# A two-layer decoder trunk on one core: the modulation product goes from VectorE to TensorE in four column groups

## The reference

```python
c_act = jax.nn.silu(c)
for l in range(DEPTH):
    mod = (c_act @ ada_w[l] + ada_b[l])[:, None, :]
    sh1, sc1, gt1, sh2, sc2, gt2 = jnp.split(mod, N_MOD, axis=-1)
    h = rms_norm(x, norm1_g[l]) * (1.0 + sc1) + sh1
    x = x + gt1 * token_mixer(h, ...)      # latent attention, differential attention, convolution, gates, w_o
    h = rms_norm(x, norm2_g[l]) * (1.0 + sc2) + sh2
    x = x + gt2 * conv_gated_mlp(h, ...)   # w_up, 3-tap convolution, silu gate, w_down
return rms_norm(x, final_g)
```

## Time and profile before

| | |
|---|---|
| median of 3 runs | 1114.99 us (1114.21 to 1120.05) |
| profiled execution | 1116.03 us, span in the trace 1114.2 us |
| TensorE busy | 1006.3 us, 90% of the span |
| VectorE busy | 869.1 us, 78% |
| ScalarE busy | 515.3 us, 46% |
| mean granted TensorE clock | 0.956 of full speed |
| DMA | 201.07 MB, 180 GB/s on average |

### The profile page before, as it was taken

One profiled execution on the slowest core, in us unless ns is written; L12 is line 12 of the kernel. 1 busy time (PEld: TensorE's weight loads), 2 busy tenths in 40 slices (PEclk: granted clock), 3 DMA queues, 4 the chain that ended last, 5 costly groups with the idle time before them and its releaser, 6 DMA issues.

```text
span 1114.2 us, 20254 instructions
## 1 busy us (share of the span) xinstructions
PE 1006.3 (90%) x7601; PEld 961.3 (86%) x7601; DVE 869.1 (78%) x1235; ACT 515.3 (46%) x715; POOL 17.3 (2%) x18
## 2 busy tenths in 40 slices
PE   2599999989888999999969999998997989999997
PEld 1598888989888999999969888898997989999996
DVE  5848989988696788898655898998869578888643
ACT  1644355437433554553345435543734355545432
POOL 6000000000000000000000000000000000000000
PEclk9898999889999899999989999987999989999998
DMA  9664443437656366657755444343666545564540
GB/s 318 239 189 152 124 131 100 153 104 249 241 195 222 115 207 221 218 188 299 265 178 187 155 124 126 105 148 109 229 232 220 185 145 199 196 218 155 187 152 38
DMA packets 138942, 201.07 MB, mean 180 GB/s; under 512 B 3416, under 2 KB 114148, under 8 KB 138852
## 3 DMA queue, kind: packets, MB, share of 16 engines
q1 hardware_dynamic: 138501, 199.63, 53.3%
q10 hardware_dynamic: 351, 0.26, 0.1%
HBM read 198.83 MB, written 1.05 MB: 179 GB/s over the span
## 4 chain that ended last, share of the span: by engine, by line
PE 62%; DVE 18%; issue 13%; ACT 2%; DMA 2%; SPq 1%; DVEq 1%; ACTq 0%
PE PB L1236 13%; PE PB L1237 12%; PE PB L1238 12%; DVE wL L838 4%; PE MI L1198 2%; PE SC L1236 2%; PE SC L1237 2%; PE SC L1238 2%; DVE buf L922 2%; DVE acc L793 2%; PE ST L1205 1%; DMA raw<-in_w_in 1%; DVE rdev L979 1%; PE SC L1337 1%; DVE xn L1025 1%
## 5 line engine op out<-in xcount | busy, mean ns | idle before, releaser
L1236 PE MATMUL PB<-hH,wH 128*128 128x256 f32 (+1 forms) x1568 | 467.8, 298 | 43.3 <-DVE hL L855 24.4
L1237 PE MATMUL PB<-hL,wH 128*128 128x256 f32 (+1 forms) x1568 | 451.8, 288 | 0.0
L1238 PE MATMUL PB<-hH,wL 128*128 128x256 f32 (+1 forms) x1568 | 451.5, 288 | 0.0
L838 DVE TENSOR_TENSOR wL<-raw,wH 128x2048 fp32r<-128x2048 f32 (+3 forms) x152 | 320.5, 2111 | 83.4 <-ACT wH L564 80.8
L1236 PEld LDWEIGHTS PB<-hH,wH 128*128 128x128 f32 (+1 forms) x1568 | 308.1, 197 | 57.2 <-issue 17.3
L564 ACT ACTIVATE wH<-raw 128x2048 fp32r<-128x2048 f32 (+3 forms) x152 | 266.4, 1769 | 132.1 <-DMA raw<-in_w_down 55.4
L1237 PEld LDWEIGHTS PB<-hL,wH 128*128 128x128 f32 (+1 forms) x1568 | 309.0, 197 | 3.3 <-issue 2.9
L1238 PEld LDWEIGHTS PB<-hH,wL 128*128 128x128 f32 (+1 forms) x1568 | 308.3, 197 | 0.0
L922 DVE SCALAR_TENSOR_TENSOR buf<-G,vec,buf 128x256 f32<-128x256 f32 x240 | 98.0, 477 | 0.3
L1075 DVE SCALAR_TENSOR_TENSOR cb<-PB,vec,cb 128x255 f32<-128x255 f32 (+1 forms) x88 | 36.3, 475 | 23.9 <-ACT cb L711 21.2
L796 DVE SCALAR_TENSOR_TENSOR acc<-ada,c_act,acc 128x1024 f32<-128x1024 f32 x40 | 51.4, 1284 | 2.3 <-DVE acc L793 1.2
(11 more groups left out here) (251 smaller groups left out, 1675.1 us busy)
## 6 DMA issues: line engine op xcount, KB each, us to landing
raw<-in_w_in SPq DMA_DIRECT2D x48, 1024.0 KB, 5.6
raw<-in_w_up SPq DMA_DIRECT2D x44, 1024.0 KB, 5.0
ada<-in_ada_w SPq DMA_DIRECT2D x40, 1024.0 KB, 5.7
raw<-in_w_down SPq DMA_DIRECT2D x22, 1024.0 KB, 5.0
ada_pre<-in_ada_w SPq DMA_DIRECT2D x8, 1024.0 KB, 11.6
raw<-in_w_o SPq DMA_DIRECT2D x8, 1024.0 KB, 6.2
raw<-in_w_out_diff SPq DMA_DIRECT2D x4, 1024.0 KB, 5.4
raw<-in_w_out_conv SPq DMA_DIRECT2D x4, 1024.0 KB, 6.0
```

Source lines behind the costliest of these rows:

```text
L838: dve.tensor_tensor(wL[s][:, 0:size], raw[s][:, 0:size], wH[s][:, 0:size].bitcast(F32), ALU.subtract).then_inc(w_lo[s], 1)
L1236: pe.matmul(out, a, xh(k), start=first and k == 0, stop=False, skip_group_check=True)
L1237: pe.matmul(out, a, xl(k), start=False, stop=False, skip_group_check=True)
L1238: ins = pe.matmul(out, b, xh(k), start=False, stop=last and k == kt - 1, skip_group_check=True)
```

## The change

The product moves to TensorE. Its weights are `c_col`, a 128x32 tile per block of rows whose column 0 holds the factors and whose other 31 columns are zero; the moving operand is the loaded block in halves of 512 columns. One load gives four matmuls, each in its own group of 32 columns of the array (`tile_position`), so each writes its own 32 partitions of `MI`; four loads accumulate there. ScalarE then copies `MI` (128x512) to `ada_rows`, and TensorE turns and adds the rows with four matmuls (`ada_rows` as weights, two columns of zeros and ones). VectorE's products, `acc` and its clearing go. VectorE still adds the bias, now near the front of a step rather than at its end. Four entries of the table move by one step, so that a part starts after the bias of the last is added. TensorE's loop over the four rounds of `w_up` is written out.

```diff
-ADA_STEPS = [1, 4, 7, 24, 26, 28, 30, 32, 34, 36, 38, 40] + [None] * 4 + [60, 62, 64, 66, 68, 70, 72, 74]
+ADA_STEPS = [1, 4, 7, 24, 27, 28, 30, 32, 35, 36, 38, 40] + [None] * 4 + [61, 62, 64, 66, 69, 70, 72, 74]
...
         @block.scalar
+            def ada_evict(count):
+                act.wait_ge(ada_used, count)
+                act.activation(ada_rows[:, :], MI[:, :], ACT.Copy).then_inc(ada_out, 1)
...
+            ada_evict(ADA_PART)
             root(0, 0)
+            ada_evict(2 * ADA_PART)
             high(0, 0)
...
             def mixer_step(l, n):
+                ada_evict_at(l, n)
                 high(l, n + 2)
...
         @block.vector
-                if first:
-                    ins = dve.tensor_scalar(acc[:, :], src[:, 0, :], factor[:, 0:1], None, ALU.mult)
-                else:
-                    ins = dve.scalar_tensor_tensor(acc[:, :], src[:, 0, :], factor[:, 0:1], acc[:, :], ALU.mult, ALU.add)
-                ins.then_inc(ada_half, 1)
-                dve.wait_ge(ada_half, halves)
-                dve.scalar_tensor_tensor(acc[:, :], src[:, 1, :], factor[:, 1:2], acc[:, :], ALU.mult,
-                                         ALU.add).then_inc(ada_used, 1)
...
                 if n < OUTS:
                     low(l, n + 2)
+                ada_work(l, n)
...
-                dve.memset(acc[:, :], 0.0).then_inc(acc_clear, 1)
...
         @block.tensor
-                for m in range(DT):
-                    ins = pe.matmul(MI[:, m:m + 1], acc[:, m * P:(m + 1) * P], ones[:, 0:1], start=True, stop=True)
+            def ada_products(src, i):
+                for k in range(2):
+                    for half in range(2):
+                        q = 2 * k + half
+                        ins = pe.matmul(MI[32 * q:32 * q + 32, :], c_col[:, 2 * i + k, :],
+                                        src[:, k, half * 512:(half + 1) * 512], start=(i == 0), stop=(i == ADA_PART - 1),
+                                        tile_position=(0, 32 * q), skip_group_check=True)
+                ins.then_inc(ada_used, 1)
+            def reduce_ada(part):
+                after(ada_out, part)
+                for m in range(4):
+                    ins = pe.matmul(MI[:, m:DT:4], ada_rows[:, m * P:(m + 1) * P], halves[:, :], start=True, stop=True,
+                                    skip_group_check=True)
+                ins.then_inc(mi_full, 1)
...
+            def ada_step(l, a):
+                after(ada_in, (l * ADA_CHUNKS + a + 1) * 16)
+                if a % ADA_PART == 0:
+                    after(mi_read, l * 6 + 2 + a // ADA_PART)
+                ada_products(ada, a % ADA_PART)
...
-                with pe.Fori(0, UP_LOOPS) as r:
+                for r in range(UP_LOOPS):
                     for j in range(4):
                         chunk(l, UP + j, r)
+                    ada_step(l, ADA_LOOP + r)
```

More of the change, by code:

```diff
@@ L238, in trunk_kernel @@
         ada = sb("ada", [P, 2, 1024])
-        acc = sb("acc", [P, 1024])
-        acc_pre = ada[:, 0, :]
+        ada_rows = sb("ada_rows", [P, 512])
+        c_col = sb("c_col", [P, DT, 32])
+        halves = sb("halves", [P, 2])
         cst = sb("cst", [P, C_MASK])
@@ L767, in _ @@
             dve.memset(half_pi[:, :], math.pi / 2)
+            link(dve.memset(halves[:, :], 0.0))
+            dve.memset(c_col[:, :, :], 0.0)
+            for q in range(4):
+                dve.memset(halves[32 * q:32 * q + 1, q % 2:q % 2 + 1], 1.0)
             dve.memset(eps[:, :], EPS).then_inc(s_ones, 1)
@@ new lines, in _ @@
+            dve.wait_ge(s_lam, 16)
+            for l in range(LAYERS):
+                ins = dve.tensor_tensor(lam_p[:, l, :, :], lam_in[:, l, 0::2, :], lam_in[:, l, 1::2, :], ALU.mult)
+            link(ins)
+            dve.tensor_reduce(lam_s[:, :, :], lam_p[:, :, :, :], AX.X, ALU.add).then_inc(s_lame, 1)
+            for l in range(LAYERS):
+                ins = dve.tensor_copy(vec_all[:, l, V_LAM:V_LAM + 2], cst[:, C_LAM + 2 * l:C_LAM + 2 * l + 2])
+            link(ins)
+            dve.wait_ge(s_lamx, 1)
@@ L831, in _ @@
+            link(dve.tensor_tensor(lamb[:, 0, :], lam_s[:, :, 1], lam_s[:, :, 0], ALU.subtract))
+            link(dve.tensor_tensor(lamb[:, 1, :], lamb[:, 0, :], vec_all[:, :, V_LAM], ALU.subtract))
             dve.wait_ge(s_vt, 1 + LAYERS)
@@ L1206, in norm_sum @@
                 ins.then_inc(st_full, 1)
+            after(s_silu, 1)
             for part in range(2):
-                if part == 1:
-                    norm_sum(0, 0)
-                after(ada_used, ADA_PART * (part + 1))
                 if part:
                     after(mi_read, part)
-                reduce_ada((acc, acc_pre)[part])
+                for i in range(ADA_PART):
+                    after(ada_pre_in[ADA_PART * part + i], 16)
+                    ada_products(ada_pre[:, ADA_PART * part + i, :, :], i)
+                if part == 0:
+                    norm_sum(0, 0)
+                reduce_ada(part + 1)
             after(s_const, 1)
@@ L1338, in attention, with ada_at @@
                     ins.then_inc(sc_full, 1)
-            def reduce_ada_at(l, n):
-                q = ADA_REDUCE_AT.get(n)
-                if q is None:
-                    return
-                def go():
-                    after(ada_used, ADA_FIRST + l * ADA_CHUNKS + ADA_PART * (q + 1))
-                    after(mi_read, l * 6 + 2 + q)
-                    reduce_ada()
-                if ADA_PARTS[q] < 2:
-                    with pe.If(l < LAYERS - 1):
-                        go()
-                else:
-                    go()
+            def ada_step(l, a):
[3 more added lines that the diff above has]
+                ada_products(ada, a % ADA_PART)
+            def ada_at(l, n):
+                q = ADA_REDUCE_AT.get(n)
+                if q is not None and ADA_PARTS[q] < 2:
+                    with pe.If(l < LAYERS - 1):
+                        reduce_ada(l * 6 + 3 + q)
+                elif q is not None:
+                    reduce_ada(l * 6 + 3 + q)
+                a = ADA_STEPS.index(n) if n in ADA_STEPS else None
+                if a is not None and a < ADA_NEXT:
+                    ada_step(l, a)
+                elif a is not None:
+                    with pe.If(l < LAYERS - 1):
+                        ada_step(l, a)
             def chunk(l, n, r=0):
```

71 lines of the change are left out of this document (19 added, 52 removed).

## The result

The change made the kernel faster: 1104.2 us median against 1117.5 for the kernel before beside it, a ratio of 0.9875 with a 95% interval from 0.9844 to 0.9905. Two repeats on two chips gave 1109.1 and 1109.5 (0.9913 and 0.9914). All 22 executions of the changed kernel lie between 1102 and 1117 us, with a median of 1108.4. I had forecast 1152 and slower. The rival on the faster side, all four groups side by side, had been given 1102.

The account below looks back on a forecast made before the run. VectorE was taken to bound the `w_up` loop, alternating with TensorE in the projections; elsewhere mostly TensorE. At 2.5 us a load, +50 for fully paid loads and smaller terms summed to +37 on 1116: 1153, 1152 beside the median; range 1098 to 1208.

Parts of the forecast that it names:

- The rival on the faster side: A load's four column groups on TensorE run wholly side by side: 1.25 us a load, sum -13, 1102 us; chance 0.18.
- the staircase of five treads: A load's eight TensorE passes: next group's first pass starts with this group's second; 2.1 us, 2.5 with shape change; chance 0.52.
- The serial rival: No passes of a load overlap on TensorE: 3.8 us a load, sum about +98, 1213 us; chance 0.17.
- paid in full, 20 loads: Loads at steps where TensorE has no hole, in both layers, each cost their whole 2.5 us: +50.
- step 6: Both layers: TensorE's 4.1 us wait for the turned keys goes, as VectorE's products ahead of them leave: -4.
- step 24: Both layers: the load costs nothing, filling TensorE's 2.6 us wait for `oAL` in step 25, blamed on a busy VectorE.
- projections 35 to 39: Output projections, both layers: VectorE loses two loads' products, 4.6 us, of which 3.5 counts as VectorE and TensorE alternate: -7.
- loop, steps 47 to 59: The `w_up` loop, eight rounds: VectorE's 25.4 us round becomes TensorE's 25.7, 23.0 plus a load: +2.4.
- waiting for a load: One buffer makes TensorE wait 1.5 us at step 28, twice, and 0.2 at each of pairs 61/62 and 69/70: +3.5.
- clock: Half-clock stretches behind TensorE's holes, as in steps 25 and 26, lessen as holes close: -9, with 0 to -18 open.
- fall behind the insertions: Rival: granted clock drops to 1.2 GHz behind inserted loads, 5 us in eight of 40 places, +40: 1190 us; chance 0.08.
- only move a wait: Rival: VectorE's products never lay in the way in the mixer; gains of steps 6, 24 and projections go: 1168; chance 0.05.

Follow-up runs that it names:

- full array: Changed kernel with no column groups: 65-column weights on the whole array, no change of array shape, same product; 1206.15 us, ratio 1.0779.
- loads spread: Changed kernel with the second part's products moved, one to step 19 and no two in neighbouring steps; 1097.26 us (0.9833), on another chip 1097.00 (0.9822).
- product at the front of a round: The version with products moved to step 19 and apart, plus each loop round's product and its transfer ahead of the four chunks; 1109.27 us (0.9913).
- in turns: Changed kernel with two column groups in place of four, matmuls issued in the order group 0, 1, 0, 1; 1141.05 us, ratio 1.0199.
- in blocks: Changed kernel with two column groups in place of four, matmuls issued in the order group 0, 0, 1, 1; 1140.98 us, ratio 1.0199.

## Why the prediction was wrong

**The step that failed** is the price of one load on TensorE, the staircase of five treads: "the second waits for the first, while the first pass of the next group [...] starts with the second pass of this one". The first half was right. The second half was not. The passes of one group are in turn, but the next group's first pass waits for nothing, and starts 7 ns behind. Two treads, 0.88 us, in place of five, 2.1. I took the row of two-pass matmuls, where the pair stands together, for a rule of the queue, although every such row used the whole array and so could not tell a queue's order from a busy array. The other part of the price, 0.4 us for the shape, measured 0.32. So a load cost 1.18 us instead of 2.5, over 40 loads 53 us, and the forecast was 1152 - 1108 = 44 too high. The difference between the two is in the relief of VectorE and the clock, below. The time lies inside the stated range, 1098 to 1208, but in the part that the range had for the side-by-side rival (chance 0.18), so the range is no support for the sum.

The serial rival was well priced: 3.8 us a load and 1213 us foreseen with 0.4 of shape change, 3.42 and 1206 measured on the full array, without one.

The other terms, with the rows of the profile after:

| term of the sum | forecast | at 1.25 a load | measured, both layers |
|---|---|---|---|
| paid in full, 20 loads | +50 | +25 | +24 (20 x 1.18) |
| step 6 | -4 | -4 | idle 4.1 us gone; with step 7, -4.3 and -1.2 |
| step 24 | 0 | 0 | steps 24 and 25: 19.65 to 15.55 us |
| projections 35 to 39 | -7 | -9 | -2.3 and -3.4 |
| loop, steps 47 to 59 | +2.4 for 8 rounds | -7 | -2.2 and -2.1; 0.68 a round, so -5.4 for 8 |
| steps 60 to 67, first layer | +6 | +1.4 | +1.3 (48.15 to 49.48) |
| a reduction | -0.95 | -0.95 | -0.7 each (9.50 to 8.83 in step 41) |
| waiting for a load | +3.5 | +3 | +2.5, all at step 28 |
| start | +4 (54) | -4.5 (46) | -3.1 (50.17 to 47.04), -2.2 and -2.3 in two more profiles |
| clock | -9 (0 to -18) | -9 | -17, -5 and -10 in three profiles, see below |

- *Paid in full.* Right in kind. Where TensorE had no hole a load lengthens its step and the next by 1.2 us together (steps 1 and 2 from 9.43 to 10.62 in both layers).
- *Step 24.* Right: the product fills part of TensorE's idle time in step 25, most of it the wait for `oAL`, 3.1 us before and 2.0 now. The gain beyond that is clock. But the prediction's reading that this wait meant a VectorE late with the products is not borne out: without them it stays as it was.
- *Projections.* The forecast reckoned with two engines in turn, and its relief was too large. The kernel without VectorE's products shows 39.6 us there, the kernel after, with three loads on TensorE, 39.1: the loads lie wholly in TensorE's waits, which shrink from 7.5 us to 3.9, and VectorE's relief is what counts. It is 1.8 and 3.1 us in the two layers even with no products at all, not 4.6 each.
- *Loop.* Right in its mechanism at either price: VectorE's round of 25.38 gives way to TensorE's, 23.0 and a load. It measures 24.70.
- *Step 28.* The wait of TensorE for `ada` that the single buffer must bring came, 1.21 and 1.26 us for the 1.5 forecast. The pairs 61/62 and 69/70 brought none.

**The clock** carried more of the result than I allowed. At 1.2 GHz two neighbouring chunk matmuls start 0.21 us apart (the kernel before, behind the start), at 2.4 GHz 0.120:

```profile
50.55 0.41 PE L1237 MATMUL PB<-hL,wH 128*128 128x256 f32 x1
50.76 0.41 PE L1238 MATMUL PB<-hH,wL 128*128 128x256 f32 x1
```

So 0.093 of 0.213, or 44%, of the time that TensorE is busy at the low clock is lost to it. The table takes that off the steps of both layers, from the first chunk matmul to the last. The last column is an estimate, worked out from the granted clock and the busy time of each profile (us):

| profile | steps | TensorE idle | busy at 1.2 GHz | steps, less 44% of that |
|---|---|---|---|---|
| before | 1048.3 | 66.5 | 72.9 | 1016.5 |
| before, loop written out | 1048.3 | 66.7 | 71.9 | 1016.9 |
| before, without VectorE's products | 1023.1 | 47.6 | 60.6 | 996.6 |
| after, first profile | 1037.5 | 40.7 | 33.3 | 1022.9 |
| after, second and third | 1050.3, 1045.5 | 41.3, 41.1 | 60.6, 49.9 | 1023.9, 1023.6 |
| after, bias at the end | 1046.6 | 41.6 | 52.4 | 1023.7 |
| loads spread, two profiles | 1035.1, 1030.6 | 35.4, 35.7 | 41.4, 30.7 | 1017.0, 1017.2 |
| product at the front of a round | 1040.2 | 38.4 | 43.0 | 1021.5 |

Profiles of one order of work agree within 1 us in the last column, though their steps differ by up to 13. By this reckoning the changed kernel does some 7 us more than the kernel before, wins 2 to 3 at the start, and is faster only because it spends less time at 1.2 GHz, which is worth 17, 5 and 10 us in its three profiles. The -9 of the sum was inside that. Nor is this chance of the profiles: the mean granted clock is 0.951 over the 51 executions of the kernel before that ran beside the experiments, and 0.966 over the 18 of the changed kernel. The stretches at 1.2 GHz that stand before in step 6 of the first layer (6.8 us) and in step 39 of both (3.4 and 6.8) are in none of the changed kernel's three profiles. The work other than clock had been set at -4 for 1.25 us a load and came out at +3 to +5, mostly because the relief of VectorE was set too large. So the rival's sum was 7 to 9 us too low, and that the first result, 1104, lies so near its 1102 is owed to the clock. The spread version does as much as the kernel before, and its whole gain over it is the clock and the start. In steps 6 and 7 the granted clock goes from 0.81 to 1.00, in 25 to 28 from 0.85 to 1.00, with idle time of 2.1 gone and of 3.1 shortened to 2.0.

The same kernel does not always get this. In its repeat the same steps, with the same order of work and holes of 3.17 and 1.96 us, were granted less (the kernel after, profiled again; steps 20 to 24, then 25 to 28):

```profile
185.11:219.25 34.14, 30.97 (x209) 28.58 (x208) 30.17 (x56) 15.80 (x26) 0.00 (x0) 0.85 0.38 121
219.25:255.73 36.48, 32.94 (x212) 28.29 (x210) 24.11 (x46) 15.76 (x28) 0.00 (x0) 0.86 0.41 132
```

70.6 us instead of 64.4, and 70.8 instead of 64.6 in the second layer: 12.4 of the 13.8 us by which the two spans of this kernel differ (1114.1 and 1100.3). That is as much as the whole change brings. What decides it, with no instruction moved, is not shown.

The other rivals: the clock did not fall behind the insertions (in the first profile no load stands within 2 us of a stretch at 1.2 GHz). The changed kernel did not only move a wait, since taking VectorE's products away alone brings 22.5 us: steps 6 and 7 go from 17.7 and 14.7 us in the two layers to 12.5 and 12.7, and the projections and the loop as shown above. At step 24 VectorE's products never made the wait, as that rival has it; the load hides in it all the same.

## What to carry to other kernels

Price a column-tiled matmul by the passes that its own group gets, plus one change of shape, and fill all four groups: here three further groups cost 0.02 to 0.03 us beside the 1.16 of the first. A row that shows two operations in order proves an order of the queue only if they could have overlapped; otherwise the range has to reach to full overlap, and the chance with it. And where TensorE's holes are followed by stretches at 1.2 GHz, count for each edit which holes it closes: moving the same products to holes brought 12 us here, 5 to 6 of them idle time and the rest clock. A transfer queued ahead of those that the path needs cost 4 to 5 us, and the version with it lost all 12, the rest by a clock that no run explains.

## What the runs showed of the hardware

- Column groups run independently of program order: four first passes start within 20 ns, second passes 0.45 us behind, and issuing two groups in turns or in blocks gives 1141.05 and 1140.98 us.
- Going from the 128-column shape to the 32-column one and back costs 0.32 us, with the weights of the next matmul, loaded only behind it, in it; a matmul of 65 columns among those of 128 costs nothing beside its passes.
- One transfer queued ahead of four others in SyncE's queue, and waiting for its buffer, delayed them by 7.5 us (8.0 less 0.5 after the start of step 40), and steps 42 and 43 by 3.2 to 3.4.
- The granted clock after one and the same hole differs between executions: 0.90 and 1.00 in steps 20 to 24 and 25 to 28 of one profile, 0.85 and 0.86 in another, 12.4 us in the two layers. A chunk matmul takes 0.213 us of TensorE at 1.2 GHz and 0.120 at 2.4, not quite twice.
